# A grid of expert weights made by adding DMAs from GpSimd in place of a one-hot matmul stage

## The reference

```python
def peer(h, w_pq, sub_keys, u_tab, v_tab):
    q = (hf @ w_pq).reshape(T, PEER_HEADS, 2, PEER_HALF)
    s = jnp.einsum('thsd,hskd->thsk', q, sub_keys)
    s_top, i_top = lax.top_k(s, PEER_TOPK)
    ...
    ids = jnp.take_along_axis(cand_i, f_pos, axis=-1)
    g = jax.nn.softmax(f_s.astype(jnp.float32), axis=-1).astype(h.dtype)
    ...
        u = jnp.take(u_tab, eb, axis=0)
        a = jax.nn.gelu(jnp.einsum('tkd,td->tk', u, xb), approximate=False)
        vv = jnp.take(v_tab, eb, axis=0)
        return jnp.einsum('tk,tkd->td', wb * a, vv)
```

## Time and profile before

| | us |
|---|---|
| median of the runs (2) | 3949.89 |
| the runs | 3949.35 to 3950.43 |
| the profiled execution | 3951.25 |
| its span | 3949.4 |
| PE busy | 3557.1 |
| DVE busy | 2771.2 |
| ACT busy | 1397.9 |
| POOL busy | 643.1 |

### The profile page before, as it was taken

The page is one execution under the profiler, slowest core; times in us unless marked ns, Lnnn a source line. Parts: engine busy times, 40 slices in busy tenths (PEclk is TensorE's granted clock), DMA queues, the critical chain, the costliest instruction groups (busy, mean ns, idle before and its releaser), DMA issues.

```text
span 3949.4 us, 49103 instructions
## 1 busy us (share of the span) xinstructions
PE 3557.1 (90%) x18246; PEld 2953.5 (75%) x18246; DVE 2771.2 (70%) x5491; ACT 1397.9 (35%) x2738; POOL 643.1 (16%) x410
## 2 busy tenths in 40 slices
PE   7877789999999857769999999999999999999996
PEld 6544435666666656659999989999888999999996
DVE  0111112666666799978888888988998898888865
ACT  1122222322222238873333333333333333333332
POOL 0000000000000000002332322332243232332302
PEclk9988889999999879989999999999999999999998
DMA  5000053334443424469999999999989999999963
GB/s 197 8 12 12 12 203 149 139 141 151 147 149 148 155 91 171 171 255 357 339 360 346 356 350 349 358 350 355 344 333 352 335 362 355 348 362 342 353 209 121
DMA packets 254913, 952.75 MB, mean 241 GB/s; under 512 B 18904, under 2 KB 119384, under 8 KB 194272
## 3 DMA queue, kind: packets, MB, share of 16 engines
q1 hardware_dynamic: 197504, 537.02, 37.2%
q0 software_dynamic: 55296, 402.68, 26.4%
q10 hardware_dynamic: 1888, 10.06, 0.6%
HBM read 888.70 MB, written 60.98 MB: 240 GB/s over the span
## 4 chain that ended last, share of the span: by engine, by line
PE 48%; DVE 5%; DMA 1%; issue 1%; ACT 0%; SPq 0%; POOLq 0%; POOL 0%; ACTq 0%; DVEq 0%
PE bank L1442 24%; PE bank L1456 24%; DMA vw<-in_v 1%; DVE ring L1544 1%; DVE accS L1561 1%; DVE uL L1621 1%; DVE vL L1616 1%; SPq L1384 0%; DVE ga L1631 0%; DVE cL L1613 0%; ACT vR L1507 0%; DVE slots L1598 0%; DVE st L1589 0%; DVE slots L1586 0%; DVE slots L1572 0%
## 5 line engine op out<-in xcount | busy, mean ns | idle before, releaser
L1407 POOL DMA_INDIRECT ring<-in_uv,slots x384 | 592.1, 1542 | 1689.5 <-DVE accS L1561 1301.2
L1442 PE MATMUL bank<-hR,uR 128*128 128x384 f32 x2048 | 692.8, 338 | 35.3 <-DVE uL L1621 35.3
L1442 PE MATMUL bank<-hR,uL 128*128 128x384 f32 x2048 | 692.2, 338 | 0.0
L1442 PE MATMUL bank<-hL,uR 128*128 128x384 f32 x2048 | 691.0, 337 | 0.0
L1561 DVE SCALAR_TENSOR_TENSOR accS<-ring,cs,accS 128x1024 f32<-128x1024 f32 x381 | 489.6, 1285 | 13.6
L1456 PE MATMUL bank<-vR,cR 128*128 128x512 f32 x1536 | 477.6, 392 | 0.7 <-DVE slots L1572 0.7
L1456 PE MATMUL bank<-vR,cL 128*128 128x512 f32 x1536 | 476.2, 391 | 0.0
L1456 PE MATMUL bank<-vL,cR 128*128 128x512 f32 x1536 | 475.9, 391 | 0.0
L1501 ACT ACTIVATE cR<-ga 128x384 fp32r<-128x384 f32 x256 | 134.6, 526 | 928.8 <-PE bank L1456 784.8
L1544 DVE CUSTOM_DVE_ANT_0 ring<-ring,slots 128x1024 f32<-128x1024 f32 x384 | 460.3, 1236 | 0.1
L1442 PEld LDWEIGHTS bank<-hR,uR 128*128 128x128 f32 x2048 | 388.5, 190 | 48.6 <-DVE uL L1621 39.0
(11 more groups left out here) (221 smaller groups left out, 4303.9 us busy)
## 6 DMA issues: line engine op xcount, KB each, us to landing
uw<-in_u SPq DMA_DIRECT2D x256, 512.0 KB
vw<-in_v SPq DMA_DIRECT2D x256, 512.0 KB
wr<-in_w_pq SPq DMA_DIRECT2D x36, 2048.0 KB, 7.7
g_scratch<-stage SPq DMA_DIRECT2D x24, 2048.0 KB, 6.3
gw<-g_scratch SPq DMA_DIRECT2D x64, 768.0 KB, 12.8
wr<-in_w_o SPq DMA_DIRECT2D x18, 2048.0 KB, 7.5
wr<-in_w_mod SPq DMA_DIRECT2D x8, 2048.0 KB, 8.1
free<-in_w_mod SPq DMA_DIRECT2D x16, 512.0 KB, 3.5
```

Of the source, the lines that this page charges most:

```text
L1407: pool.indirect_dma_start(out=ring[:, k % R, :], out_offset=None, in_=a["uv"], in_offset=bass.IndirectOffsetOnAxis(ap=ids[:, k // P, k % P ...
L1442: mm = pe.matmul(A[t][:, 0:CW], w[:, t, k, :], h[:, k, :], start=(k == 0 and w is uR and h is hR), stop=(k == DK - 1 and w is uL))
```

## The change

`weigh` is gone. The grid is now two DRAM tensors of 16384 x 384 floats. POOL writes zeros over both (64 stores of 768 KB) in `mixer_inputs`, once the modulation is made. `middle` converts a dense tile's ids to cell numbers, and POOL adds each weight to its cell by an indirect DMA with an addition: one DMA for each of a tile's 128 token slots, with 128 addresses and 4 bytes each. The 16 of one head form a group; a group waits until the same tile's previous group has landed, since two heads may hit one cell. `wavefront` sorts the 48 groups; 26 are issued in `middle`, and 22 in the first sweep of `experts`, one every five steps ahead of that step's gathers. The dense tiles are now 0 to 5 and the sparse ones 6 to 8; the latter are turned back to token-major form in `middle` (`back`). `gw` is loaded as one run of 6 KB a partition in place of 12 runs of 512 B.

```diff
-TB = 32
-CB = CW // TB
 UB = 4
-U = 8
 SW = D + 2 * P
-STILES = (0, 1, 2)
-DENSE = ((3, 4, 5), (6, 7, 8))
+STILES = (6, 7, 8)
+DENSE = ((0, 1, 2), (3, 4, 5))
 NS = len(STILES)
-NDB = len(DENSE) * CB
+ND = len(DENSE)
+GRID = NE * CW
+ZW = 1536
+NZ = ND * GRID // (P * ZW)
+EARLY = 26
+
+
+def wavefront():
+
+    place = {}
+    for d in range(ND * CT):
+        for h in range(PH):
+            place[d, h] = (4 * d if d < CT else 18 + d) + 2 * h
+    return sorted(place, key=lambda dh: (place[dh], dh[0]))
+
+
+GROUPS = wavefront()
...
-        g_dram = nc.dram_tensor("g_scratch", [NDB, P, NKEY, TB], F32, kind="Internal").ap()
+        g_dram = [nc.dram_tensor(f"g_scratch{n}", [GRID, 1], F32, kind="Internal").ap() for n in range(ND)]
...
-            mixer_inputs(nc, a, sb, sem, PS, ident, modc, sp1, silu, slots, krT, kT, vv)
-            middle(nc, a, sb, sem, PS, ident, modc, sp1, silu, slots, krT, kT, vv, x1_dram, gate_dram)
-        weigh(nc, a, sb, sem, PS, ident, slots, g_dram)
-        experts(nc, a, sb, sem, PS, slots, x1_dram, g_dram, gate_dram)
-
-
-def mixer_inputs(nc, a, sb, sem, PS, ident, modc, sp1, silu, slots, krT, kT, vv):
+            mixer_inputs(nc, a, sb, sem, PS, ident, modc, sp1, silu, slots, krT, kT, vv, g_dram)
+            placed = [sem(f"g_placed{d}") for d in range(ND * CT)]
+            middle(nc, a, sb, sem, PS, ident, modc, sp1, silu, slots, krT, kT, vv, x1_dram, gate_dram, g_dram, placed)
+        experts(nc, a, sb, sem, PS, slots, x1_dram, g_dram, gate_dram, placed)
+
+
+def place(pool, slots, g_dram, placed, d, h):
+
+    i = DENSE[d // CT][d % CT]
+    if h:
+        pool.wait_ge(placed[d], h * TOPK * 16)
+    for k in range(h * TOPK, (h + 1) * TOPK):
+        pool.indirect_dma_start(
+            out=g_dram[d // CT][:, :],
+            out_offset=bass.IndirectOffsetOnAxis(ap=slots[:, i, D + k:D + k + 1].bitcast(U32), axis=0),
+            in_=slots[:, i, D + PAIRS + k:D + PAIRS + k + 1], in_offset=None,
+            compute_op=ALU.add).then_inc(placed[d], 16)
...
+        zero = free[:, 2 * D:2 * D + ZW]
...
+                pool.wait_ge(mod_ready, 1)
+                pool.memset(zero, 0.0).then_inc(zero_set, 1)
+                pool.wait_ge(zero_set, 1)
+                for b in range(NZ):
+                    if b >= 4:
+                        pool.wait_ge(zeroed[b % 4], b // 4 * 16)
+                    n, at = b % ND, b // ND * P * ZW
+                    pool.dma_start(g_dram[n][at:at + P * ZW, :].rearrange("(p c) o -> p (c o)", p=P),
+                                   zero).then_inc(zeroed[b % 4], 16)
+                for k in range(4):
+                    pool.wait_ge(zeroed[k], NZ // 4 * 16)
...
+            if i - 2 in STILES:
+                number("back", i - 2, 0)
+                number("back", i - 2, 1)
...
+                pool.iota(cell0[:, :], pattern=[[P, CT]], base=0, channel_multiplier=1,
+                          allow_small_or_imprecise_dtypes=True).then_inc(cell_ready, 1)
+                for d, h in GROUPS[:EARLY]:
+                    pool.wait_ge(routed, DENSE[d // CT][d % CT] + 1)
+                    place(pool, slots, g_dram, placed, d, h)
...
+                def back(i, half):
+                    ps = bank("back", i, half)
+                    for k in range(4):
+                        at = (4 * half + k) * P
+                        mm = pe.transpose(ps[:, k * P:(k + 1) * P], slots[:, i, at:at + P], ident[:, :])
                     mm.then_inc(w_mm, 1)
...
+                        if i - 2 in STILES:
+                            back(i - 2, 0)
+                            back(i - 2, 1)
...
+                def back(i, half):
+                    ps, f = bank("back", i, half)
+                    act.activation(slots[:, i, half * 512:(half + 1) * 512], ps[:, :], ACT.Copy).then_inc(f, 1)
...
-                    ids = slots[:, i, DK * P:DK * P + PAIRS]
-                    dve.scalar_tensor_tensor(ids.bitcast(U32) if i in STILES else ids, out[:, 0, :], float(NKEY),
-                                             out[:, 1, :], ALU.mult, ALU.add)
+                    ids = slots[:, i, D:D + PAIRS].bitcast(U32)
+                    if i in STILES:
+                        dve.scalar_tensor_tensor(ids, out[:, 0, :], float(NKEY), out[:, 1, :], ALU.mult, ALU.add)
+                    else:
+                        d = [x for row in DENSE for x in row].index(i)
+                        if d == 0:
+                            dve.wait_ge(cell_ready, 1)
+                        ch.step(dve.scalar_tensor_tensor(cell[:, :], out[:, 1, :], float(NKEY), out[:, 0, :],
+                                                         ALU.mult, ALU.add))
+                        dve.tensor_scalar(ids, cell[:, :], float(CW), cell0[:, d % CT:d % CT + 1], ALU.mult, ALU.add)
                     dve.wait_ge(e_out, i + 1)
                     ch.step(dve.tensor_reduce(hm[:, :], ex[:, :, :], axis=AX.X, op=ALU.add))
                     ch.step(dve.reciprocal(hi[:, :], hm[:, :]))
-                    ch.step(dve.tensor_tensor(
+                    dve.tensor_tensor(
                         slots[:, i, DK * P + PAIRS:].rearrange("p (h k) -> p h k", h=PH), ex[:, :, :],
-                        hi[:, :].rearrange("p (h o) -> p h o", o=1).to_broadcast([P, PH, TOPK]), ALU.mult))
+                        hi[:, :].rearrange("p (h o) -> p h o", o=1).to_broadcast([P, PH, TOPK]),
+                        ALU.mult).then_inc(routed, 1)
+                    dve.wait_ge(routed, i + 1)
...
-def weigh(nc, a, sb, sem, PS, ident, slots, g_dram):
...
-        gw = sb(c, "gw", [P, 2, CB, UB, TB])
+        gw = sb(c, "gw", [P, 2, UB, CW])
...
-        gate_1 = slots[:, 3:7, D:]
-        ids = slots[:, 0:NS, D:D + PAIRS].bitcast(U32)
+        gate_1 = slots[:, 0:4, D:]
+        ids = slots[:, STILES[0]:STILES[0] + NS, D:D + PAIRS].bitcast(U32)
+        grid = [g[:, :].rearrange("(p c) o -> p (c o)", p=P) for g in g_dram]
...
-                        sp.dma_start(gw[:, b % 2, :, :, :].rearrange("p c u t -> p c (u t)"),
-                                     g_dram[n * CB:(n + 1) * CB, :, m:m + UB, :].rearrange(
-                                         "c p u t -> p c (u t)")).then_inc(g_in[b % 2], 16)
-                    if g == NEt // 2:
+                        if m == 0:
+                            for d in range(n * CT, (n + 1) * CT):
+                                sp.wait_ge(placed[d], PAIRS * 16)
+                        sp.dma_start(gw[:, b % 2, :, :].rearrange("p u t -> p (u t)"),
+                                     grid[n][:, m * CW:(m + UB) * CW]).then_inc(g_in[b % 2], 16)
+                    if g == NEt - 16:
                         sp.wait_ge(h_l, 2)
+                        sp.wait_ge(placed[CT], PAIRS * 16)
...
+                late = GROUPS[EARLY:]
                 for k in range(R):
                     gather(k)
                 for g in range(GT):
+                    if g % 5 == 0 and g // 5 < len(late):
+                        place(pool, slots, g_dram, placed, *late[g // 5])
...
-                        gv = ga[:, x % 2, :].rearrange("p (c t) -> p c t", c=CB)
-                        dve.tensor_tensor(gv, gv, gw[:, x // UB % 2, :, x % UB, :], ALU.mult).then_inc(c_f, 1)
+                        gv = ga[:, x % 2, :]
+                        dve.tensor_tensor(gv, gv, gw[:, x // UB % 2, x % UB, :], ALU.mult).then_inc(c_f, 1)
```

More of the change, by code:

```diff
@@ L114, in build, with mixer_inputs @@
             vv = big[:, KT * H * P:2 * KT * H * P].rearrange("p (t c) -> p t c", t=KT)
-            mixer_inputs(nc, a, sb, sem, PS, ident, modc, sp1, silu, slots, krT, kT, vv)
-            middle(nc, a, sb, sem, PS, ident, modc, sp1, silu, slots, krT, kT, vv, x1_dram, gate_dram)
-        weigh(nc, a, sb, sem, PS, ident, slots, g_dram)
-        experts(nc, a, sb, sem, PS, slots, x1_dram, g_dram, gate_dram)
-def mixer_inputs(nc, a, sb, sem, PS, ident, modc, sp1, silu, slots, krT, kT, vv):
+            mixer_inputs(nc, a, sb, sem, PS, ident, modc, sp1, silu, slots, krT, kT, vv, g_dram)
[12 more added lines that the diff above has]
+            compute_op=ALU.add).then_inc(placed[d], 16)
+def mixer_inputs(nc, a, sb, sem, PS, ident, modc, sp1, silu, slots, krT, kT, vv, g_dram):
     with ExitStack() as c:
@@ L164, in mixer_inputs @@
         hs = [hT[:, :, :], hT1]
+        zero = free[:, 2 * D:2 * D + ZW]
+        zeroed = [sem(f"a_zero{k}") for k in range(4)]
+        zero_set = sem("a_zset")
         cl, wl = sem("a_small"), sem("a_weights")
@@ L461, in _, with middle @@
                 finish(pe, NT - 1)
-def middle(nc, a, sb, sem, PS, ident, modc, sp1, silu, slots, krT, kT, vv, x1_dram, gate_dram):
+def middle(nc, a, sb, sem, PS, ident, modc, sp1, silu, slots, krT, kT, vv, x1_dram, gate_dram, g_dram, placed):
     NH = NT * H
@@ L565, in middle @@
         out = sb(c, "out", [P, 2, PAIRS])
+        cell = sb(c, "cell", [P, PAIRS])
+        cell0 = sb(c, "cell0", [P, CT])
```

(10 more changed lines are left out.)

144 lines of the change are left out of this document (removed).

## The result

| | us |
|---|---|
| before, median of the runs | 3949.89 |
| after, median of 2 runs (4071.66 to 4078.2) | 4074.93 |
| ratio, 95% interval | 1.0317, 1.0272 to 1.0361 |
| the profiled execution of after | 4071.66 (span 4069.8) |

The account below looks back on a forecast made before the run. PE was taken to bound the first sweep, with DVE close behind. 3655.1 without the stage, + 17 (zeros) + 5 (middle block) + 28 (adds in the sweep) = 3705, so 3704 us as median; range 3650 to 4030.

Parts of the forecast that it names:

- What goes, -296.1: Between middle block and experts: removing the stage `weigh` takes 296.1 us off the path, leaving 3655.1.
- The zeros, +17: In the mixer: zero stores are covered, but about three `xt` loads land late beside them, +17 us (ends 0 and 50).
- The middle block, +5 for `back` and the decoding: Middle block: transposes ahead of query matmuls and one more short DVE instruction per dense tile, +5 us (ends 0, 12).
- The price of an adding DMA: POOL's time per add, read from the gather: 1.4 us in the middle block, 1.6 beside the sweep (ends 1.24, 2.8).
- the forecast's line: Middle block: 368 adds run without a hole from 863.7 us, at 1.4 each ending at 1379, before 1453.8.
- the cover: Middle block: time until its end at 1453.8 us that hides POOL's adds, used up at 1.60 us an add.
- the walk: First sweep: adds stepped along DVE's instruction starts, each waiting for the one in work; 5 per paired step, 1.6 us each.
- The adds in the first sweep, +28: First sweep: POOL just keeps up, 40.3 of 41.5 us; late gathers cost 6.3 us in a fifth of 22 groups, +28.
- The DMA queues, 0: First sweep: adding packets need 4.2 us per engine and group against 3.6 free, about even; nothing charged.
- rival C: First sweep: DMA engines short of time, 0.1 to 0.15 us an adding packet, 3878 to 4019 us; within near-no-change chance 0.17.
- B: Both covers: an addition needs a second read, up to 1.88 us; 4073 to 4288 us, slower; chance 0.22 including C's far end.
- A: Both covers a little short: an add costs 1.85 us, middle block +91, sweep +62, 3829 us; chance 0.15.

Follow-up runs that it names:

- The last run: The changed kernel without any adding DMA and with the zero stores timed to avoid the `xt` loads and one small store: 3655.61 us, ratio 0.9251 to before.

## Why the prediction was wrong

**What goes, -296.1: right.** The last run gives it within 2 us.

**The zeros, +17: right in size, in part by luck.** The middle block starts 17.1 us late. Of this `xt` has some 10 and ACT's wait for its own `new_krope` store 6 to 7. The forecast spoke of `xt` only, took three loads at 5.7 for it, and missed the store.

**The middle block, +5 for `back` and the decoding: 0.** The lateness at its end (16.0) is no more than at its start (17.1).

**The price of an adding DMA: this step failed, and it decided the sign.** The gather was taken as the nearest row and its 0.94 us as the price of 128 addresses. That reading holds for a plain scatter (0.985 in the middle block, 1.30 beside the sweep). The addition puts 0.61 us on top of it: 1.596 and 1.966 in the mean, 1.90 and 2.27 with the gap, where 1.4 and 1.6 stood in the sum. In the middle block the forecast's line with 1.90 gives 863.7 + 368 x 1.90 = 1562.9, 109 past the block's end. 127.5 was measured. The line itself began too early: 863.7 is the first routing write plus the mean interval of 84.2, but the trace before has the second write 95.8 us after the first:

```profile
779.18 0.29 DVE L1100 TENSOR_TENSOR slots<-ex,hi 128x128 f32<-128x128 f32 x1
874.94 0.29 DVE L1100 TENSOR_TENSOR slots<-ex,hi 128x128 f32<-128x128 f32 x1
```

That is 11 us, and by the same line the cover ended at (1453.8 - 874.9) / 368 = 1.57 us an add and not at 1.60. The rest is 2 us of waits for a group before and 5 us from POOL's last add to the first load. Beside the sweep the price is 0.66 us above the plain scatter's, 10.6 a group, and the run with plain scatters is 189 us shorter in `experts` than after is, 8.6 a group. One part of the price was taken too high, not too low: the walk let each descriptor run wait for any DVE instruction in work, and with it the forecast took 1.4 in the middle block, where the plain scatter took 0.985 + 0.30 = 1.29.

**The adds in the first sweep, +28: failed a second time, by its form.** Even at the price assumed the sweep loses 84 us, as the plain scatter shows. The step compared the lateness of one gather (4.6 us) with the rest that DVE has in five steps (5.0) and took the rest for a cover. But the next group stands on POOL's queue behind a pair that DVE has to release, so what is late once starts the next turn late as well. The numbers were there to close the circle: group 25.6, second gather 2.2, landing 9.1, and from the earlier trace rows 4.1 to DVE's sum, 1.6 until POOL's next pair, 3.8 for that pair: 46.4 us against 41.5, 108 us in 22 groups where 84 were measured. A rest of DVE stands in none of these terms.

**The DMA queues, 0: right as far as it was tried.** 38 ns a packet, not 100 to 150 as rival C needed, and the share of the queues in the sweep fell. But wherever adds ran beside the sweep, POOL's rate or the circle held it, so the pace forecast was not tried: at 144 packets a DMA a group brings an engine 144 x 38 ns = 5.5 us (an estimate), against the 3.6 that the forecast had free in 41.5 us. Nor is it being small that makes such a packet dear: those of the plain scatter, 18 bytes each in the mean, took 12 ns.

**The rivals.** B is what happened, at the low end of its 4073 to 4288, and that its total came so near is luck. Its reason, a second descriptor per element, would have made up to 1.88 us of 0.94, and 1.54 came. Its two parts were off in opposite ways, 127 where it had 216 and 273 where it had 181 at that price, since it too had the sweep bound by POOL's rate and not by the circle. A had the price of the middle block nearly (1.85), and its +91 there came from that; its sweep of 62 failed like the forecast's.
The Trainium skill, "Collectives: The Full Stack", section "The bandwidth ceiling: the fold count and why AG ≠ RS ≠ AR", has two read descriptors for a transfer that reduces. By this rule alone an add would take twice the plain time; the trace agrees in direction, 1.54 against 0.95 beside an idle DVE, a factor of 1.6. Whether the 0.6 us are spent on those descriptors no run here shows.

(A slip that changes little: 8 gathers go in 15.0 us by the pairs of the earlier trace rows, 1.86 + 1.29 and two gaps of 0.30 a pair; the 14.7 are the mean of the earlier trace rows.)

The chance for slower was 0.22, nearly all of it B. A price that no row shows, for the one new instruction of which there are 768, deserved more: by its own line 0.2 us more on each used the cover up.

## What to carry to other kernels

Before a queue gets new work ahead of old, close the circle: add up the time from the new work, through what waits behind it, the engine that uses that, and back to the place from which the new work starts again. If the sum is longer than the period, each turn loses about the difference, however much rest any one engine has; cutting the work up, with the old work first, gave back 111 of 273 us here. And where a change rests on a count times a price that no row shows, ask at which price the cover ends: here that was 1.57 us, and one operation with and without the addition would have told.

## What the runs showed of the hardware

- An indirect DMA of 128 addresses from GpSimd takes 0.95 us as a plain scatter and 1.54 with an addition, at the least, and 0.30 lie before the next one.
- Beside DVE's work in the sweep both grow, to means of 1.30 and 1.97 us. The Trainium skill, "SBUF — State Buffer", section "Who interferes with whom", has DVE instructions with two SBUF inputs contend with a GpSimd instruction that reads SBUF; the trace agrees, with adds of 1.54 us while DVE waited (2248.17) and up to 2.62 in the sweep. In the middle block, where DVE is busy for 69% of the time too, an add takes 1.60 in the mean and mostly 1.54. Two adds there: the first lies mostly beside a DVE instruction with one such tile as its input (`r`, with columns of scalars), the second beside two instructions with two. POOL's rows, then DVE's:

```profile
1111.08 1.54 POOL L140 DMA_INDIRECT g_scratch<-slots  x1 [0.30 <-issue]
1112.93 1.95 POOL L140 DMA_INDIRECT g_scratch<-slots  x1 [0.30 <-issue]
```

```profile
1111.39 0.81 DVE L1086 TENSOR_SCALAR r<-r,mv,rs 128x1024 f32<-128x1024 f32 x1
1112.24 1.23 DVE L1087 TENSOR_TENSOR r<-r,ln_g 128x1024 f32<-128x1024 f32 x1
1113.50 1.22 DVE L1088 TENSOR_TENSOR xr<-r,ln_b 128x1024 f32<-128x1024 f32 x1
```

- The queue of the plain scatters from 900 to 1370 us (359 of them), in the form of the earlier trace rows:

```profile
q0 software_dynamic: 11424, 0.21, 1.8%
```

  That is 32 packets a DMA and 12 ns each (0.018 x 470 x 16 / 11424), where 263 adding ones from 900 to 1400 us made 37,850, 144 each at 38 ns. So an addition also takes some 14 times the time of the DMA engines, 5.5 us summed over them against 0.4.
- A store of 32 KB, issued 2 us after the first of four stores of 768 KB from another queue, landed in 8.3 us where it took 1.6.
